# Loading the input and C in other shapes, with the rotation doublings on the vector engine

## What is computed

```python
xn = _rmsnorm(h, g_mix[0])
ab = exp(lam * dt)                       # complex, per group and state
bb = (ab - 1) / lam * b                  # input matrix, from b_re, b_im
h  = associative_scan(ab, bb @ u)        # over positions
y  = c_re @ h_re - c_im @ h_im + d * u   # C: (64 groups, 16, 64)
z  = gelu(y)
gl = z @ w_glu + b_glu
h  = h + gl[:, :1024] * sigmoid(gl[:, 1024:])
```

## Time and profile before

| what | value |
|---|---|
| time, median of 3 runs | 1419.99 us (1419.76 to 1420.94) |
| the profiled execution | 1419.51 us, of which the span in the trace is 1417.7 us |
| PE busy | 1333.3 us, 94% of the span |
| DVE, ACT, POOL busy | 733.9, 444.8, 784.7 us |
| first large matmul (L879) starts | 152.12 us |

### The profile page before, as it was taken

How to read it: one execution, slowest core, us unless ns; L and a number is a source line. 1 busy time by engine, 2 the same in 40 slices (tenths; PEclk the granted TensorE clock), 3 DMA queues, 4 the chain that set the end, 5 groups by cost and what they waited for, 6 DMA issues and landing times.

```text
span 1417.7 us, 28729 instructions
## 1 busy us (share of the span) xinstructions
PE 1333.3 (94%) x10956; PEld 1293.5 (91%) x10956; DVE 733.9 (52%) x1276; ACT 444.8 (31%) x951; POOL 784.7 (55%) x699
## 2 busy tenths in 40 slices
PE   2569899999999999999999987999999999999998
PEld 2558799999999999999999954999999999999998
DVE  7788533455555551233768766555555555212254
ACT  2744211234343322101242276224333333110021
POOL 3880456555555665555655455445666655555552
PEclk9989999999999999999999999999999999999999
DMA  5034433233322233223553220322223333332322
GB/s 110 4 74 105 96 88 87 75 89 89 89 86 83 85 104 91 85 85 107 112 128 96 60 83 1 99 77 85 83 85 88 89 89 100 89 88 86 93 90 67
DMA packets 228951, 121.18 MB, mean 85 GB/s; under 512 B 25245, under 2 KB 227824, under 8 KB 228508
## 3 DMA queue, kind: packets, MB, share of 16 engines
q1 hardware_dynamic: 217688, 107.78, 26.9%
q10 hardware_dynamic: 11196, 12.46, 4.1%
HBM read 115.18 MB, written 7.07 MB: 86 GB/s over the span
## 4 chain that ended last, share of the span: by engine, by line
PE 84%; DVE 6%; ACT 5%; ACTq 2%; issue 2%; POOL 0%; DMA 0%; SPq 0%; DVEq 0%; POOLq 0%
PE ACC L879 57%; PE MI L879 10%; PE SS L879 9%; PE MI L708 3%; ACTq L1327 1%; ACT PB L1749 1%; PE SS L1215 1%; DVE T L2023 1%; DVE RSTD L2093 1%; ACT XN L1279 1%; DVE PB L2308 1%; PE SS L1093 1%; DVE T L2017 1%; ACT PTR L1279 0%; PE ACC L1030 0%
## 5 line engine op out<-in xcount | busy, mean ns | idle before, releaser
L655 POOL TENSOR_TENSOR SPL<-RAW,SPL 128x1024 fp32r<-128x1024 f32 (+2 forms) x172 | 450.0, 2616 | 14.3
L879 PE MATMUL ACC<-NH,SPL 128*128 128x272 f32 x2016 | 344.4, 289 | 0.7 <-DVE AL L2154 0.7
L652 POOL TENSOR_TENSOR TIC<-EPSB 128x1 f32<-128x1 f32 x172 | 37.0, 215 | 534.7 <-PE ACC L879 342.7
L879 PEld LDWEIGHTS ACC<-NH,SPL 128*128 128x128 f32 x2016 | 286.9, 188 | 1.8 <-issue 0.9
L879 PE MATMUL ACC<-AH,SPL 128*128 128x272 f32 x1408 | 237.5, 289 | 0.0
L879 PE MATMUL ACC<-NL,SPL 128*128 128x272 f32 x1008 | 207.9, 288 | 0.0
L879 PEld LDWEIGHTS ACC<-AH,SPL 128*128 128x128 f32 x1408 | 198.9, 188 | 0.2
L653 POOL TENSOR_SCALAR SPL<-RAW 128x1024 fp32r<-128x1024 f32 (+2 forms) x172 | 195.7, 1138 | 0.2 <-issue 0.2
L879 PEld LDWEIGHTS ACC<-NL,SPL 128*128 128x128 f32 x1008 | 158.4, 188 | 0.0
L879 PE MATMUL ACC<-AL,SPL 128*128 128x272 f32 x704 | 145.3, 287 | 0.0
L1804 DVE SCALAR_TENSOR_TENSOR ACC<-WK,CP,ACC 128x560 f32<-128x560 f32 x88 | 70.9, 806 | 97.2 <-ACT ACC L1279 90.8
(11 more groups left out here) (350 smaller groups left out, 2004.7 us busy)
## 6 DMA issues: line engine op xcount, KB each, us to landing
RAW<-in_w_up_dram SPq DMA_DIRECT2D x88, 512.0 KB
RAW<-in_w_down_dram SPq DMA_DIRECT2D x32, 704.0 KB
RAW<-in_w_glu_dram SPq DMA_DIRECT2D x16, 512.0 KB
RAW<-in_w_ple_gate_dram SPq DMA_DIRECT2D x16, 512.0 KB
KT<-bias_rows SPq DMA_DIRECT2D x64, 64.0 KB, 2.5
RAW<-in_w_q_dram SPq DMA_DIRECT2D x16, 256.0 KB
RAW<-in_w_o_dram SPq DMA_DIRECT2D x32, 128.0 KB
RAW<-in_w_ple_in_dram SPq DMA_DIRECT2D x16, 128.0 KB
```

What stands on the lines that cost most here:

```text
L652: PIN.tensor_tensor(TIC[:], EPSB[:], EPSB[:], ALU.add)
L655: PIN.tensor_tensor(lo, RAW[:, u, 0:kt, :], hi.bitcast(F32), ALU.subtract).then_inc(sem("split_done"), 1)
L879: last = mm(out[:, h, :], SPL[:, u, w, w0 + k, :], x[:, k0 + k, HT * h:HT * h + HT], start=start and k == 0 and n == 0, stop=stop and k == ...
```

## The change

It has five parts.

1. x comes in four transfers of 64 rows, two positions each, with a semaphore each (`x_pair0` to `x_pair3`), issued after the samples. ACT squares positions 2i and 2i+1 as soon as pair i is there.
2. C is loaded as it lies in memory, in two transfers of 32 rows of 8 KB (`CN`), both from SP, after `x_pair2`. PE turns it with 64 small products [32 x 64] by the identity [32 x 32], in place of 8 transposes [128 x 128]. ACT's 8 transfers of C are gone, and SP's 8 become 2. `CN` lies where `CA` is written later, and `CA` is now copied when both halves are turned.
3. The six doublings of the unit numbers (30 instructions) go from POOL to DVE, between `powers_in` and `BC`; the semaphore `turns_ready` is gone.
4. In the GLU, ACT loads the sigmoid's table with a one-column activation right after `VSO`, and does the first sigmoid and the first `high_square` before it issues the stores and loads.
5. The stores, `CST`, `PST`, `RB` and `OHB` are issued after these and before `gate(1)`.

```diff
-            sp.wait_ge(sem("x_first"), 64)
-            for t in range(4):
-                for a in range(2):
-                    sp.dma_start(CS_[:, 1, t, 64 * a:64 * a + 64],
-                                 ssm_c_im[0].rearrange("(t q a) c s -> t a q c s", t=4, a=2)[t, a]).then_inc(sem("c_in"), 16)
+            sp.wait_ge(sem("x_pair2"), 16)
+            for r, src in enumerate((ssm_c_re, ssm_c_im)):
+                sp.dma_start(CN[:, r].rearrange("q a c s -> q (a c s)"),
+                             src[0].rearrange("(q a) c s -> q (a c s)", a=2)).then_inc(sem("c_in"), 16)
...
             pool.wait_ge(sem("powers_in"), 1)
-            for lv in range(6):
-                t = TURNS + 3 * lv
-                w = A4_RE + 2 if lv == 0 else t - 3
-                PIN.tensor_tensor(PR[:, X4:X4 + 2, :], PR[:, w:w + 2, :], PR[:, w:w + 2, :], ALU.mult)
-                chain.link(PIN.tensor_tensor(PR[:, X6, :], PR[:, w, :], PR[:, w + 1, :], ALU.mult))
-                PIN.tensor_tensor(PR[:, t, :], PR[:, X4, :], PR[:, X5, :], ALU.subtract)
-                PIN.tensor_tensor(PR[:, t + 2, :], PR[:, X4, :], PR[:, X5, :], ALU.subtract)
-                last = PIN.tensor_tensor(PR[:, t + 1, :], PR[:, X6, :], PR[:, X6, :], ALU.add)
-                if lv < 5:
-                    chain.link(last)
-            last.then_inc(sem("turns_ready"), 1)
-            pool.wait_ge(sem("turns_ready"), 1)
             pool.wait_ge(sem("c_turned"), 2)
...
-            pe.wait_ge(sem("c_in"), 256)
+            pe.wait_ge(sem("c_in"), 32)
             for r in range(2):
-                for t in range(4):
-                    last = turn(ACC[:, r, P * t:P * t + P], CS_[:, r, t, :], P)
-                last.then_inc(sem("c_made"), 1)
-
-            pe.wait_ge(sem("x_first"), 64)
-            pe.wait_ge(sem("x_in"), 48)
+                for c in range(CG):
+                    for a in range(2):
+                        last = mm(ACC[64 * a:64 * a + 64, r, PAIRS * c:PAIRS * c + PAIRS], CN[:, r, a, c, :],
+                                  IDN[0:PAIRS, 0:PAIRS], start=True, stop=True, skip_group_check=True)
+            last.then_inc(sem("c_made"), 1)
+
+            for i in range(4):
+                pe.wait_ge(sem("x_pair%d" % i), 16)
+            pe.wait_ge(sem("x_in"), 32)
...
             act.wait_ge(sem("lam_in"), 48)
-            for i in range(4):
-                act.dma_start(XS[NSEQ:64, 2 * i:2 * i + 2, :], chunks[0:64 - NSEQ, 2 * i:2 * i + 2, :]).then_inc(sem("x_first"), 16)
             act.dma_start(XS[0:NSEQ, 0:STEPS, :], x_sample).then_inc(sem("x_in"), 16)
             act.dma_start(XS[NU_:NC_, STEPS:CH, :], x_sample).then_inc(sem("x_in"), 16)
             act.wait_ge(sem("xz_set"), 1)
-            act.dma_start(XS[64:NU_, :, :], chunks[64 - NSEQ:64]).then_inc(sem("x_in"), 16)
-            for t in range(4):
-                for a in range(2):
-                    act.dma_start(CS_[:, 0, t, 64 * a:64 * a + 64],
-                                  ssm_c_re[0].rearrange("(t q a) c s -> t a q c s", t=4, a=2)[t, a]).then_inc(sem("c_in"), 16)
+            for i in range(4):
+                act.dma_start(XS[NSEQ:NU_, 2 * i:2 * i + 2, :], chunks[:, 2 * i:2 * i + 2, :]).then_inc(sem("x_pair%d" % i), 16)
...
             for j in range(CH):
+                if j % 2 == 0:
+                    act.wait_ge(sem("x_pair%d" % (j // 2)), 16)
...
+            act.wait_ge(sem("c_made"), 1)
             for r in range(2):
-                act.wait_ge(sem("c_made"), r + 1)
-                copy(CA[:, r, :, 0, :], ACC[:, r, :].rearrange("p (q c) -> p q c", c=CG), scale=1.0 - 2.0 * r).then_inc(sem("c_turned"), 1)
+                copy(CA[:, r, :, 0, :], ACC[:, r, :].rearrange("p (c q) -> p q c", q=PAIRS), scale=1.0 - 2.0 * r).then_inc(sem("c_turned"), 1)
...
+            nc.scalar.activation(TIC2[:], EPSB[:], ACT.Sigmoid)
...
+            act.wait_ge(sem("strip_done"), 1)
+            act.wait_ge(sem("z_split"), KC)
+            A(halves(SG), acc(0), ACT.Sigmoid, bias=VEC[:, V_BGLU + KC:V_BGLU + KC + 1]).then_inc(sem("glu_taken0"), 1)
+            high_square("n1", 0, V_GFFN, NH, True)
+
             act.wait_ge(sem("fs_out"), 1)
...
             act.dma_start(RB[0:NBUCK, :], rel_bias).then_inc(sem("rb_dma"), 16)
             act.dma_start(OHB[:], consts[0:NBUCK + 1, C_OH:C_OH + BW]).then_inc(sem("rb_dma"), 16)
...
-            act.wait_ge(sem("strip_done"), 1)
-            act.wait_ge(sem("z_split"), KC)
-            A(halves(SG), acc(0), ACT.Sigmoid, bias=VEC[:, V_BGLU + KC:V_BGLU + KC + 1]).then_inc(sem("glu_taken0"), 1)
-            high_square("n1", 0, V_GFFN, NH, True)
             gate(1)
...
+            for lv in range(6):
+                t = TURNS + 3 * lv
+                w = A4_RE + 2 if lv == 0 else t - 3
+                T(PR[:, X4:X4 + 2, :], PR[:, w:w + 2, :], PR[:, w:w + 2, :], M_)
+                link(T(pr(X6), pr(w), pr(w + 1), M_))
+                T(pr(t), pr(X4), pr(X5), S_)
+                T(pr(t + 2), pr(X4), pr(X5), S_)
+                link(T(pr(t + 1), pr(X6), pr(X6), A_))
             dve.wait_ge(sem("g_copied"), 1)
```

More of the change, by code:

```diff
@@ L257, in build @@
         UZ = ph1("UZ", [P, NBL, NC_])
+        ca_at = ph1.at
         CA = ph1("CA", [P, 2, PAIRS, CH + 1, CG])
@@ L266, in build @@
         ZTK = ph1("ZTK", [P, CH, P])
+        CN = nc.alloc_sbuf_tensor_at("CN", [PAIRS, 2, 2, CG, 64], F32, offset=ca_at)
         BC = nc.alloc_sbuf_tensor_at("BC", [P, 2, PAIRS, CG], F32, offset=hsv_at)
@@ L271, in build @@
         stg = Region(uz_at)
-        CS_ = stg("CSTG", [P, 2, 4, P])
         LAMS = stg("LAMS", [64, P])
@@ L1323, in _ @@
             act.wait_ge(sem("xz_set"), 1)
-            act.dma_start(XS[64:NU_, :, :], chunks[64 - NSEQ:64]).then_inc(sem("x_in"), 16)
-            for t in range(4):
-                for a in range(2):
-                    act.dma_start(CS_[:, 0, t, 64 * a:64 * a + 64],
-                                  ssm_c_re[0].rearrange("(t q a) c s -> t a q c s", t=4, a=2)[t, a]).then_inc(sem("c_in"), 16)
+            for i in range(4):
+                act.dma_start(XS[NSEQ:NU_, 2 * i:2 * i + 2, :], chunks[:, 2 * i:2 * i + 2, :]).then_inc(sem("x_pair%d" % i), 16)
             act.wait_ge(sem("g_made"), 1)
             copy(GS[:], SS[:, 1, :]).then_inc(sem("g_copied"), 1)
-            act.wait_ge(sem("x_first"), 64)
-            act.wait_ge(sem("x_in"), 48)
+            act.wait_ge(sem("x_in"), 32)
             act.wait_ge(sem("xs_zero"), 1)
             for j in range(CH):
+                if j % 2 == 0:
+                    act.wait_ge(sem("x_pair%d" % (j // 2)), 16)
                 if j >= 2:
@@ L1473, in _ @@
             copy(VSO[:].rearrange("p r h n -> p (r h n)"), MI[:, 0, :]).then_inc(sem("fs_out"), 1)
[L1474 to L1478, removed]
             def load_ffn(l):
@@ L1503, in _ @@
             high_square("n1", 0, V_GFFN, NH, True)
+            act.wait_ge(sem("fs_out"), 1)
+            for r, (dp, ds_) in enumerate(((ssm_re_p, ssm_re_s), (ssm_im_p, ssm_im_s))):
+                store(dp[0, 0].rearrange("(q a) s -> q (a s)", a=2), FSO[:, r, :])
+                for h in range(2):
+                    store(ds_[0, 4 * h:4 * h + 4].rearrange("b (q a) s -> (b q) (a s)", a=2), VSO[:, r, h, :])
+            act.wait_ge(sem("fs_ready"), 1)
+            load_ffn(0)
+            act.dma_start(RB[0:NBUCK, :], rel_bias).then_inc(sem("rb_dma"), 16)
+            act.dma_start(OHB[:], consts[0:NBUCK + 1, C_OH:C_OH + BW]).then_inc(sem("rb_dma"), 16)
             gate(1)
@@ L1978, in _ @@
             dve.wait_ge(sem("uz_made"), len(XG))
-            dve.wait_ge(sem("turns_ready"), 1)
             nc.vector.memset(EROT[:, 0, :, NB // 2:NB // 2 + 1], 1.0)
```

## The result

| kernel | median us (range, runs) | ratio to before, 95% interval |
|---|---|---|
| before, timed beside it | 1420.57 (1419.20 to 1422.08, 15) | |
| after | 1416.90 (1414.63 to 1419.41, 15) | 0.9974 [0.9966, 0.9982] |

The change makes the kernel 3.7 us faster (2.6 to 4.8 by the interval). The forecast was 10.4 us faster, with a range that ended at 5.1; the direction is right, the size is not. The profiled execution of after took 1417.46 us, its span is 1415.4, 2.3 less than the span before.

What follows compares the result with a forecast made beforehand. PE, busy 94%, was taken as the bound, with the start gated by the copies into CA. Start -10.4 us plus GLU 0 took the median 1419.99 to 1409.6 us, range 1406.4 to 1414.9.

Steps and rivals of the forecast that it cites:

- The twelve microseconds of issuing, the pairs, the squares: Start: ACT copies GS by 10, x's pairs land at 12.8, 15.4, 18.0 and 20.6, root at 24.3 us.
- that rival: Start: x's pairs don't land one by one but all near 20.6; S = 6.3, 1413.7 us; chance 0.08.
- C's landing: Start: SP issues C's two transfers at 18.0 and 18.4; with 4.2 us to land, C is there at 22.5.
- I take 3.8: PE's turning of C: 64 small products at 0.059 us each take 3.8 us, so C is turned at 26.3.
- products at the transposes' pace: Rival on turning C: 7.5 us for 64 products, turned at 30.0; S = 6.7, 1413.3 us; chance 0.12.
- S: Start: how much earlier the copies into CA end, the gate for ACT, PE and POOL; forecast 10.4 us.
- So S reaches 152.12 whole: Start to first large product at 152.12: no other engine eats the gain, so all 10.4 us arrive there.
- The doublings: DVE before BC: 0.77 us a level, 4.6 in all, covered by its wait; BC at 25.2, reciprocal at 37.2.
- DVE becomes the bound: Rival in the start: doublings cost 7.5 us, reciprocal comes at 40.1; S = 8.3, 1411.7 us; chance 0.08.
- The sigmoid: GLU: sigmoid done by 163.7 in before's clock, so PE no longer waits 2.45 us.
- This part gives back what it wins: 0: GLU: 2.4 us won, then PE waits 2.2 at L916 for RB and OHB behind PST; net 0, from -2.4 to +1.2.
- a lateness of 3 to 5 us more at L916: Rival in the GLU: RB and OHB land 3 to 5 us later still, 1413 to 1415 us; chance 0.06.

Runs made afterwards that it cites:

- e6: e1 with C loaded one group a row and turned by 32 one-instruction transposes, four copies into CA: 1411.19 us.
- e4: After with 32 products in place of 64 to turn C, odd channels being copies of even ones: 1414.30 us.
- e9: After with both RB and OHB issued ahead of the stores and 32 products in place of 64 for C: 1408.76 us.
- e3: Before with ACT's new order in the GLU alone: 1424.11 us.
- e10: Before with ACT's new GLU order, and RB and OHB issued ahead of the stores: 1418.71 us.
- e1: After with RB and OHB issued ahead of the stores, CST and PST: 1411.92 us.
- e2: After with ACT's old GLU order put back, stores and loads before the first sigmoid: 1414.26 us.
- e7: e1 with the doublings put back on GpSimd: 1411.23 us.
- e5: After with 16 small products into an unused bank ahead of PE's wait for RB and OHB: 1415.85 us.
- e8: e1 with SP issuing C after x's first pair, not the third: 1413.39 us.

## Why the prediction was off, point by point

- **The twelve microseconds of issuing, the pairs, the squares: right.** GS ended at 10.09 (by 10). The pairs were taken up at 14.15, 18.85 and 21.39; pairs 2 and 3 were forecast to land at 18.0 and 20.6, so about 0.8 early. Pair 0 was taken up 1.3 later than its 12.8. They land one by one, and that rival is out. The root came at 24.95 to 25.25 against 24.3. The Trainium skill ("DMA: Bandwidth & Descriptors", "Why a DMA increments its semaphore by 16 and not by 1") says that a copy uses the largest number of engines up to 16 that divides its rows. The trace agrees: with the samples on 8 engines, as that gives, pair 2 was forecast at 18.0, spread evenly it would have come 1.3 earlier, and it came at 18.83.
- **C's landing: right within 1 us.** Issued at 18.84 and 19.20 (18.0 and 18.4), landed at 23.4 (22.5), 4.2 after issue, as forecast.
- **"I take 3.8": the step that failed.** The 64 products took 7.03. The earlier trace rows was read as 32 products in 1.90 us, 0.059 each. It is 32 instructions, and the code has 16 products there (4 x 2 x 2): this f32 product appears in the trace as two instructions, where a transpose is one (BN's 32 transposes are x32, e6's 32 are x16 twice). The rows before showed it too: the code has one product at L916, and the earlier trace rows has it as x2. Read so, says 0.119 a product, 7.6 for 64, and BN's transposes 7.5: both rows gave the upper bound and nothing was left for the lower one. The rival "products at the transposes' pace" (S = 6.7, 0.12) was the case: S is 6.1 at PE and 6.2 at POOL. e4 measures the term by itself, e9 gives it back whole. The Trainium skill ("FP8 and Floating Point Precision", "TensorE Precision Notes") says that true FP32 takes four passes through the array; the rows show two instructions a product, and nothing here shows what happens inside one.
- **"So S reaches 152.12 whole": nearly.** 6.12 at PE's second block, 6.2 at XN (42.38 against 48.56), 5.73 at the first large product. The 0.4 is no more than executions differ by. From POOL's first power of C to the first large product it is 114.15 us in before, 114.58 in after, and 113.87 and 114.64 in e3 and e10, which have before's start. Their `V` in the first scans takes 2.0 to 2.1 us once in before and e3 and twice in after and e10; that this is the cause was not tried.
- **The doublings: right.** 20.57 to 25.32, 0.79 a level (0.77), BC at 25.32 (25.2), the reciprocal at 37.34 (37.2), XN not held up. DVE still has 4.97 us idle ahead of DGV, and 1.94 in e4 with its S of 9.2 (the forecast left 0.8 at 10.4), so "DVE becomes the bound" is out.
- **The sigmoid: right.** Done at 158.1, the 2.45 us are gone in after and worth 2.7 in e10.
- **"This part gives back what it wins: 0": the second step that failed.** The cause was named in the prediction (RB and OHB last in ACT's queue, behind PST), and e1 shows that their place is it. The Trainium skill ("DMA: Bandwidth & Descriptors", "Queues, rings and completion order") says that each engine takes a queue's work in ring order. That agrees with OHB landing at 176.46, 8.36 us after its issue and behind PST's 175.6 in after, and with no wait once it goes first, which e1's earlier issue would explain as well. The size was off in two ways: the wait is 3.39, not 2.2, and it doesn't end with itself. The clock fell in it, which cost 0.65 in the small product and 1.9 in the next strip, a term that the sum didn't have. That the landing itself was only 0.9 off (182.2 in before's clock, not 181.3) is luck: OHB went out 1.5 us earlier than forecast (173.8, not 175.3) and took 8.4 us, not 6.0. Part net: -3.5 by the trace, -3.5 alone in e3.

The parts add up by the medians: start 6.3 (e2), sigmoid 2.7 (e10), together 9.0 against 8.7 in e1; start and the GLU as made, 6.3 - 3.5 = 2.8 against 3.7 in after. With intervals of 2 us this agrees, and shows no more than that. From the forecast's 10.4 go 3.2 for the turning (7.03 - 3.8), 0.9 for C's landing, 0.4 on the way to the first large product and 3.5 for the GLU: 2.4 is left, and the two spans differ by 2.3.

Both steps that failed stood among the rivals, each by itself: the slow products with 1413.3 (0.12), a lateness of 3 to 5 us more at L916 with 1413 to 1415 (0.06). The first came as described. Of the second the size came (3.5 us lost), but 2.6 of it by the clock and only 1.2 by a wait longer than the forecast's 2.2. The two together had no price; so the measured 1416.90 lies above the range's end of 1414.9. Two small sums of the prediction are off and touch nothing: an S of 11.2 with a wait of 0.8 gives 1407.4, not 1408, and a landing 20 us after PST's issue 1421.8, not 1421.6.

The best version that turns C whole is e1 (or e6, e7, equal within the measurement): 8.7 to 9.6 us faster than before, 5 to 6 faster than after.

## What to carry to other kernels

Count instructions and products apart: divide a row's time by the number of calls in the code, not by its x, before it is used as a price. A small transfer that someone waits for goes to the head of its queue when the issues around it are moved; issuing CST some 10 us later was harmless (e10: at 174.93, before at 164.48), being the last of the eleven issues was not. A wait on the engine that is the bound costs more than its length if the clock falls behind it, so price it with the strip that follows, and judge such a kernel by medians of several runs.

## What the runs showed that was not expected

- A wait of PE of 2.5 to 3.4 us was followed by a granted clock of 0.50 to 0.57 over a stretch of 4 us in after, e2, e3 and e4, and by none in the profile of before, where the same wait of 2.45 left 96 matmuls at 12.29 us (13.61 in e2). It cost 1.3 us on top of the wait in e2, 1.5 in e3, 2.6 in after and 2.7 in e4 (a wait of 2.96, then 1.46 for the small product). What decides whether the clock falls is not shown.
- The clock was also low where no edit reached. In seven profiles (e1, e2, e3, e5, e6, e7, e10) the GLU's first 36 matmuls took 6.27 to 6.29 us at a granted clock of 0.70 to 0.87 in the stretches of 4 us there; in the other five it was 1.00 and they took 4.75 to 4.76. So the profile of e1 carries 1.5 us that those of before and after do not, and it is not laid beside them end to end.
- PE filled with small products kept 1.00 (e5).
- The same stretch of small products took 1.95 us at full clock and 3.67 at 0.50 in executions of nearly the same kernel (e4, e9); the runs of one kernel differ by up to 5.7 us (e10), and how much of that is the clock is not shown.
- Two transfers issued 4.9 us earlier landed 1.3 us later (the second took 10.8 us from issue to landing in e8, 4.6 in e1), and x's last pair came 2.1 us later.
